# Two hundred and sixty-four matmuls with alternating streams behind the last panel of a transformer block kernel

## The reference

```python
h = h + gla_mixer(rmsnorm(h) , w_in, ...)        # gated linear attention
h = h + relu(rmsnorm(h) @ w_up) ** 2 @ w_down    # hidden width 8192
x = rmsnorm(h)
proj = rmsnorm(x) @ w_in_2                       # 6144 columns
y = concat(stick_breaking_attention(q, k, v) * silu(g), rg_lru(conv(x_lru)) * silu(g_lru))
out = x + y @ w_out_2                            # 2048 x 2048
```

## Time and profile before

| | us |
|---|---|
| median of the runs shown (1503.52 and 1505.21) | 1504.37 |
| the profiled execution, whole | 1504.49 |
| the profiled execution, its span | 1502.7 |
| TensorE busy in it | 1494.1 |
| mean granted TensorE clock, share of full | 0.998 |

### The profile page before, as it was taken

How to read it: one execution, slowest core, us unless ns; L and a number is a source line. 1 busy time by engine, 2 the same in 40 slices (tenths; PEclk the granted TensorE clock), 3 DMA queues, 4 the chain that set the end, 5 groups by cost and what they waited for, 6 DMA issues and landing times. The chain is left out here.

```text
span 1502.7 us, 17691 instructions
## 1 busy us (share of the span) xinstructions
PE 1494.1 (99%) x7210; PEld 1252.8 (83%) x7210; DVE 854.3 (57%) x889; ACT 719.4 (48%) x858; POOL 23.8 (2%) x44
## 2 busy tenths in 40 slices
PE   8999999999999999999999999999999999999999
PEld 7788888888888888888888888888888888888887
DVE  5555545555556545655555655565656776565654
ACT  5543544445544433444344433444554664565632
POOL 1000000000000000000000000000000011000000
PEclk9999999999999999999999999999999999999999
DMA  9444465557555555555555555555555455544563
GB/s 328 151 157 163 144 198 179 184 179 240 188 187 187 196 190 189 191 186 196 194 184 196 185 194 196 186 192 189 186 173 180 155 194 189 165 152 159 183 221 124
DMA packets 77760, 279.16 MB, mean 186 GB/s; under 512 B 8704, under 2 KB 9216, under 8 KB 77296
## 3 DMA queue, kind: packets, MB, share of 16 engines
q1 hardware_dynamic: 75744, 273.06, 54.5%
q0 software_dynamic: 784, 3.08, 0.7%
q10 hardware_dynamic: 1152, 1.90, 0.4%
HBM read 275.91 MB, written 2.10 MB: 185 GB/s over the span
## 5 line engine op out<-in xcount | busy, mean ns | idle before, releaser
L1006 DVE TENSOR_TENSOR w_lo<-raw,w_hi 128x1024 fp32r<-128x1024 f32 x508 | 620.5, 1225 | 601.0 <-ACT w_hi L709 599.8
L709 ACT ACTIVATE w_hi<-raw 128x1024 fp32r<-128x1024 f32 x508 | 536.8, 1059 | 720.2 <-PE banks L403 503.4
L401 PE MATMUL banks<-w_hi,xa 128*128 128x512 f32 x752 | 301.1, 400 | 0.5 <-DVE w_lo L1006 0.5
L401 PE MATMUL banks<-w_hi,xb 128*128 128x512 f32 x768 | 299.6, 390 | 0.0
L403 PE MATMUL banks<-w_hi,xb 128*128 128x512 f32 x768 | 298.9, 389 | 0.0
L402 PE MATMUL banks<-w_lo,xb 128*128 128x512 f32 x768 | 298.8, 389 | 0.0
L403 PE MATMUL banks<-w_hi,xa 128*128 128x512 f32 x752 | 294.3, 391 | 0.0
L402 PE MATMUL banks<-w_lo,xa 128*128 128x512 f32 x752 | 294.1, 391 | 0.0
L425 PE MATMUL banks<-xa,w_hi 128*128 128x512 f32 x1024 | 256.4, 392 | 0.0
L425 PEld LDWEIGHTS banks<-xa,w_hi 128*128 128x128 f32 x1024 | 184.4, 189 | 33.1
L403 PEld LDWEIGHTS banks<-w_hi,xb 128*128 128x128 f32 x768 | 144.2, 188 | 29.9
(11 more groups left out here) (196 smaller groups left out, 612.8 us busy)
## 6 DMA issues: line engine op xcount, KB each, us to landing
raw<-in_weights SPq DMA_DIRECT2D x511, 512.0 KB, 3.3
h<-in_x SPq DMA_DIRECT2D x2, 1024.0 KB, 11.6
arena<-in_x_turned SPq DMA_DIRECT2D x7, 256.0 KB, 6.5
result<-stage ACTq DMA_DIRECT2D x6, 256.0 KB, 4.5
arena<-in_final_norm POOLq DMA_DIRECT2D x1, 1024.0 KB, 7.6
raw<-in_weights SPq DMA_DIRECT2D x2, 256.0 KB, 4.1
arena<-in_gla_b_gate POOLq DMA_DIRECT2D x1, 512.0 KB, 9.3
arena<-in_lru_w_a POOLq DMA_DIRECT2D x1, 512.0 KB, 10.0
```

Of the source, the lines that this page charges most:

```text
L401: pe.matmul(o, xh[:, kt, xs], w_hi[:, slot, k, :], start=kt == 0, stop=False)
L709: act.activation(w_hi[:, n % RING, :, :], raw[:, n % RING, :, :], ACT.Copy)\
L1006: dve.tensor_tensor(w_lo[:, n % RING, :, :], raw[:, n % RING, :, :], w_hi[:, n % RING, :, :].bitcast(F32), ALU.subtract).then_inc(lo_ready, 1)
```

## The change

`measure(tiles, streams)` is added behind the last panel, inside TensorE's program. It issues 12 matmuls; number i takes its tile and its stream from the lists in turn and writes to bank 4 + i % 4, as wide as the stream. It is called 22 times, and nobody reads what it writes.

The tiles are blocks of `xb`'s high part (`tiles`) or of `w_hi` (`weights_as_tiles`). A stream is a view of a slot of `w_hi` (`flat`, 1024 numbers) or of a block of `xb` (`pairs`, 2 x 256 numbers). Most views are turned so that the last index steps between distant places: `woven` takes number b of the first half of a slot, then number b of the second half, 2 KB on, for b from 0 to 255. `pitch(w)` takes two neighbouring runs of w numbers and alternates between them (distance 4w bytes: 1 KB for 256 down to 16 bytes for 4), then the next two runs. The `step` lines alternate between two slots at 4, 8 or 12 KB, the views with `a=4` and `a=8` among four or eight places, and the last ones use `xb`. Two views are plain runs of neighbours: `"p a b -> p (a b)"` (512 columns) and `p[:, 0, :]` (256 columns).

```diff
--- before.py
+++ after.py
@@ -684,6 +684,42 @@
             keep_running(34)
             for t in range(PANELS):
                 run(t)
+
+            def measure(tiles, streams):
+
+                for i in range(12):
+                    stream = streams[i % len(streams)]
+                    width = 1
+                    for d in stream.shape[1:]:
+                        width *= d
+                    o = banks[:, 4 + i % 4, 0:width]
+                    pe.matmul(o, tiles[i % len(tiles)], stream, start=True, stop=True)
+
+            tiles = [xb[:, i, 0, 0:P] for i in range(12)]
+            weights_as_tiles = [w_hi[:, i, 0, j * P:(j + 1) * P] for i in range(RING) for j in range(4)]
+            flat = [w_hi[:, i, :, :].rearrange("p a b -> p (a b)") for i in range(RING)]
+            pairs = [xb[:, i, :, :] for i in range(8)]
+            woven = [f.rearrange("p (a b) -> p b a", a=2)[:, 0:S, :] for f in flat]
+
+            def pitch(w):
+                return [f[:, 0:N].rearrange("p (c a b) -> p c b a", a=2, b=w) for f in flat]
+
+            measure(tiles, woven)
+            measure(tiles, woven)
+            for w in (256, 128, 64, 32, 16, 8, 4):
+                measure(tiles, pitch(w))
+            for step in (1, 2, 3):
+                measure(tiles, [w_hi[:, 0:step + 1:step, 0, 0:S].rearrange("p a b -> p b a")])
+            measure(tiles, [f.rearrange("p (a b) -> p b a", a=4)[:, 0:P, :] for f in flat])
+            measure(tiles, [f[:, 0:N].rearrange("p (a b) -> p b a", a=4) for f in flat])
+            measure(tiles, [f.rearrange("p (a b) -> p b a", a=8)[:, 0:64, :] for f in flat])
+            measure(weights_as_tiles, [p.rearrange("p a b -> p b a") for p in pairs])
+            measure(weights_as_tiles, [p.rearrange("p a b -> p (a b)") for p in pairs])
+            measure(weights_as_tiles, [p.rearrange("p h (a b) -> p h b a", a=2) for p in pairs])
+            measure(weights_as_tiles, [p[:, 0, :] for p in pairs])
+            measure(weights_as_tiles, [p[:, 0, :].rearrange("p (a b) -> p b a", a=2) for p in pairs])
+            measure(weights_as_tiles, [f.rearrange("p (a b) -> p b a", a=2)[:, 0:P, :] for f in flat])
+            measure(tiles, woven)
 
 
         def panel_done(eng, t):
```

## The result

The changed kernel takes 1559.78 us (median of 1559.33 and 1560.24), against 1504.37 us before: a ratio of 1.037, 95% interval 1.034 to 1.040. It is slower, as was forecast, and by more than a measurement can mistake, but by 55 us and not by 98. The range of 1553 to 1630 holds it. (In the kernel's text `KINDS` stands at line 36 and `first_bank` at line 71, a few lines from where the description above puts them.)

What follows compares the result with a forecast made beforehand. TensorE's instruction stream, busy 1494.1 of 1502.7 us, was taken as the bound. First new start 1499.09 + X 101.4 + 0.16 last record + 0.4 program end + 1.79 outside the span gave 1602.8 us; 8-in-10 range 1553 to 1630.

Steps and rivals of the forecast that it cites:

- free alternation: Rival for the added streams: alternating places cost no more than a run; X 52.9 to 56.0, time 1554.3 to 1557.4; chance 0.27.
- the form of the sum: Program end: time = 1501.44 + X, with the old tail hidden beneath the new matmuls.
- X: Time of the 264 new matmuls behind the last panel, from start to start; forecast 101.4 us.
- C and D: Added plain runs: 12 matmuls of 512 columns and 12 of 256; 2.7 + 1.4 = 4.1 us.
- A and B: Added alternating streams: 216 matmuls of 512 columns and 24 of 256; forecast 92.2 + 5.1 = 97.3 us.
- half the rate: Main forecast for alternating streams: 0.427 us per 512 columns, 0.2135 per 256; time 1602.8 us, chance 0.42 with the falling clock.
- The lower bound X = 52.9: Added matmuls if alternation lifts the run's limit to the array's pace, 0.214 us a pass; alternating streams then 48.8 us.
- By distance: Rival for alternating streams: only some distances collide, others are free; X 78.7, time 1580.1 us; chance 0.15.
- A price of 0.85 and more: Rival for alternating streams: a whole access paid for each column; X from 199.1, time 1700.5 or 1712.3; chance 0.14 above half rate.
- The falling clock: Rival: stalled streams count as idle, so all new matmuls run at clock 0.50; time 1606.4; chance inside the forecast's 0.42.
- Every added matmul was executed: Denies the rival that unread new matmuls are not executed, leaving the time at 1504.4 us; that rival's chance 0.02.
- L: Later theory, from the experiments: columns dealt in turn to two lanes, each keeping one aligned 16-byte piece; each change costs 0.885 ns.

Runs made afterwards that it cites:

- e2_kinds: Instead of the change's groups, 22 groups of 12 matmuls behind the last panel, varying number format, tile and bank; a bfloat16 run took 0.2158 us a matmul.
- e3_weights_in_turn: Kernel before, no added matmuls; panels not of kind u stored even columns first and streamed in turn from two halves; 1459.01 us, ratio 0.9696.
- e4_u_too: As e3_weights_in_turn, with kind u panels' streams alternating between token halves and kinds d and D taking every second token as tile; 1436.54 us, ratio 0.9546.
- e1_places: Instead of the change's 22 groups, 45 groups of 12 matmuls behind the last panel, varying places, turns and steps; run 0.2267 us, two places 0.2158 us a matmul.

## Why the prediction was right and where it failed

**The time: right, and in part by luck.** The direction was right, and 1559.8 lies in 1553 to 1630. But the range reached that low only because it was stretched to take in free alternation; the forecast's own range, 1602 to 1609, misses by 42 us, and the mechanism with the chance of 0.42 is not the one that the trace shows.

**What bounds the kernel, and the form of the sum: right.** The new work is added whole, no wait and no idle time before it, the clock stays at 1.00, and VectorE and SyncE are hidden. With the measured X the sum gives 1559.80, against a median of 1559.78. Its small terms are less exact than that: in the profiled execution (1559.33) the first new matmul starts at 1498.79 and not 1499.09, 0.3 us and not 0.4 lie behind the last one, and 1.73 and not 1.79 outside the span, 0.5 us together.

**C and D: right**, 2.7 and 1.4 us as measured. The tile loads cost nothing, as said.

**The price of A and B: wrong, and this is the step that failed.** I took 0.427 us, "half the rate", because "a reader with no slack should not serve two places as fast as one". Measured: 0.2158 us for two places, 180 of the 216 matmuls of A, and 0.1117 for B; only four places (0.283) and eight (0.487) cost more than a run. X was mis-sized by 101.4 - 58.4 = 43 us. The premise, that reading sets the pace of a float32r run, is borne out: the run takes 0.2267, while two places and a bfloat16 run (e2_kinds), with half the bytes, both take 0.2158. The inference was wrong. I pictured one reader that has to jump; the runs fit two, each fed by every second column, for which a run is the awkward case and two places are the easy one. The lower bound X = 52.9 had been worked out from the very row that shows this slack, full float32's 0.4275 a record, and would have been nearly right for two places alone (0.214 against 0.2158).

**The rivals.** Free alternation (0.27) is what 17 of the 20 alternating groups show; its X of 52.9 to 56.0 falls short of 58.4 by the three groups of four and eight places. By distance (0.15): from 16 bytes to 12 KB the price of two places does not move (8, 12 and 20 bytes, tried later, do cost more), and its X of 78.7 is 20 us too high. A price of 0.85 and more occurs for no float32r stream here; the largest is 0.55. The falling clock did not come here, but it is no idle fear: in e2_kinds the granted clock fell to 0.50 with TensorE busy without a gap, under bfloat16 streams of up to 0.865 us. Every added matmul was executed.

**The rule of the Trainium skill.** Every second column of one place costs 0.451 us, twice a run, so a stream that leaves a piece early does pay, as the Trainium skill's SBUF — State Buffer, Specifications (TRN2), has it. But by that section of the Trainium skill two hits on a 16-byte line are enough for full bandwidth; here two used columns of each four cost 0.451 in one place and 0.2273 in two, and all four, in a run, cost 0.2267 where two places reach 0.2158. The measurements decide: the rows fit a count of which columns a lane gets. The Trainium skill's TensorE: Matmul & The Clock Gate, Back-to-back issue gap, is right with its N/2.4 + 2.5 ns for two places (128 to 512 columns) and for the bfloat16 run of 512, and 5% short for a float32r run of 512.

**What stays open.** Why four places cost 0.283 and turns of 2 and 4 neighbours 0.340 and 0.252, between keeping one piece and keeping two. Why turns of 8 to 32 neighbours cost 0.237 to 0.243 where L counts 0.2267, and eight and more places up to 0.550, over the most that L can count. Why distances of 12 and 20 bytes cost more than the count of changes. Why bfloat16 from two places costs 0.484. Full float32 would fit theory L if each number passes twice in a row (a run like each column twice, two places like turns of 2 or four places, four like eight), but nothing was run to test that. The lanes themselves are a model that counts the prices of one and two places, not something that a trace shows.

## What to carry to other kernels

A float32r stream of neighbouring columns runs 5% below the array's pace on this chip; taken in turn from two places a multiple of 16 bytes apart (16 bytes to 12 KB were tried; 8, 12 and 20 bytes cost more) it runs at full pace. An order chosen when the weights are laid out makes that free, 1505.3 to 1459.0 us here, and to 1436.5 us with the activations' streams turned too. Plain steps of two and more columns double the price, and more than two places cost 24% to 155% over two. To price an access pattern that no row shows, measure a dozen matmuls of it behind the real work, with the granted clock beside them: from the prices taken there, e3_weights_in_turn and e4_u_too came out 5 us over what was expected, with gains of 46 and 69, and the one with four places 15 us under, in 311.

## What the runs showed of the hardware that was not expected

- Two places cost less than a run: 0.2158 against 0.2267 us for 512 columns of float32r, at distances of 16 bytes to 12 KB, all multiples of 16 bytes.
- The loss of a run varies: one column on 0.2368, sixteen on 0.229, 64 on 0.2267 us, and the same run from column 0 0.2267 in one place of the program and 0.230 in another; two places move by at most 1 ns.
- bfloat16 behaves the other way round: a run 0.2158, two places 0.484, four 0.865 us; the 0.865 is the same at a granted clock of 1.00 and of 0.50.
- The granted clock can fall while TensorE is busy all the time: to 0.50 near 1533 us in e2_kinds, behind bfloat16 streams of 0.484 and 0.865 us. Beside float32r streams of 0.43 to 0.55 us (e1_places) it stayed at 1.00.
- A tile loaded by every second column takes 194 ns instead of 188, though the same step doubles a stream's price; by every fourth column it takes 0.33 us and shows, 0.237 instead of 0.2158 a stream.
